# Sample attention of a streaming encoder: head-by-head products in four 32-column groups, keys turned three half-streams ahead

## The reference

```python
def diff_attn_sample(q, k_new, v_new, cache_k, cache_v, lam):
    s_past = jnp.einsum('bqhcd,bkhcd->bhcqk', q, cache_k)      # 512 cached keys per stream
    s_new = jnp.einsum('bqhcd,bkhcd->bhcqk', q, k_new)         # 16 new keys
    p = jax.nn.softmax(jnp.concatenate([s_past, s_new], axis=-1), axis=-1)
    a = p[:, :, 0] - lam * p[:, :, 1]                          # the two maps c = 0, 1
    return (jnp.einsum('bhqk,bkhv->bqhv', a[..., :P], cache_v)
            + jnp.einsum('bhqk,bkhv->bqhv', a[..., P:], v_new))
```

## Time and profile before

| | us |
|---|---|
| median of three runs | 3280.58 |
| span of the profiled execution (the page gives no other time of it) | 3277.7 |
| PE busy | 3119.9 (95%) |
| PE weight loads busy | 2657.1 (81%) |
| DVE busy | 1301.2 (40%) |
| ACT busy | 853.0 (26%) |
| POOL busy | 767.1 (23%) |
| of the chain that ended last: PE | 31% of the span |
| of it L1645, L1610, L1597, L1629, L1617 (the sample stage) | 2%, 2%, 1%, 1%, 0% |

### The profile page before, as it was taken

One profiled execution on the slowest core, in us unless ns is written; L12 is line 12 of the kernel. 1 busy time (PEld: TensorE's weight loads), 2 busy tenths in 40 slices (PEclk: granted clock), 3 DMA queues, 4 the chain that ended last, 5 costly groups with the idle time before them and its releaser, 6 DMA issues. The chain is left out here.

```text
span 3277.7 us, 40419 instructions
## 1 busy us (share of the span) xinstructions
PE 3119.9 (95%) x15436; PEld 2657.1 (81%) x15436; DVE 1301.2 (40%) x2469; ACT 853.0 (26%) x1712; POOL 767.1 (23%) x895
## 2 busy tenths in 40 slices
PE   8999899899999999999998898899899999999997
PEld 6978577789998899978886777666678998899996
DVE  2156744532222222265224767633253222222226
ACT  2152331222211122221012555522123221122212
POOL 1112111421222121242121533412042211211214
PEclk9999888999999999999997988999898999999998
DMA  4102305111111111112224323253211111111111
GB/s 130 39 26 68 106 15 204 33 52 39 45 45 38 39 51 38 45 33 74 100 90 113 89 70 73 97 206 141 99 52 40 51 39 45 45 38 38 45 32 58
DMA packets 234007, 219.68 MB, mean 67 GB/s; under 512 B 78209, under 2 KB 178434, under 8 KB 233874
## 3 DMA queue, kind: packets, MB, share of 16 engines
q1 hardware_dynamic: 233874, 217.91, 21.1%
HBM read 184.83 MB, written 33.03 MB: 66 GB/s over the span
## 5 line engine op out<-in xcount | busy, mean ns | idle before, releaser
L1243 PE MATMUL ps<-xt,wsplit 128*128 128x384 f32 x5184 | 911.3, 336 | 2.4 <-DVE xt L1681 2.4
L1243 PEld LDWEIGHTS ps<-xt,wsplit 128*128 128x128 f32 x5184 | 907.8, 189 | 5.3 <-issue 2.0
L707 POOL TENSOR_TENSOR wsplit<-raw,wsplit 128x1024 fp32r<-128x1024 f32 x192 | 461.6, 2405 | 1837.6 <-ACT wsplit L881 1837.6
L1414 PE MATMUL ps<-wsplit,hT 128*128 128x512 f32 x3456 | 787.9, 390 | 0.0
L1414 PEld LDWEIGHTS ps<-wsplit,hT 128*128 128x128 f32 x3456 | 649.4, 188 | 134.1
L1261 PE MATMUL ps<-wsplit,xt 128*128 128x512 f32 x3024 | 703.6, 394 | 2.8 <-DVE xt L1681 2.8
L1261 PEld LDWEIGHTS ps<-wsplit,xt 128*128 128x128 f32 x3024 | 571.4, 190 | 128.4 <-issue 6.5
L881 ACT ACTIVATE wsplit<-raw 128x1024 fp32r<-128x1024 f32 x192 | 202.4, 1054 | 970.3 <-PE ps L1414 612.9
L1887 DVE TENSOR_TENSOR x_res<-x_res,ps 128x512 f32<-128x512 f32 x252 | 172.4, 687 | 439.3 <-PE ps L1414 439.3
L1920 DVE TENSOR_SCALAR hsq<-ps 128x384 f32<-128x384 f32 x192 | 107.1, 558 | 558.9 <-PE ps L1243 558.9
L1024 ACT ACTIVATE hsq<-hsq 128x384 f32<-128x384 f32 x192 | 101.1, 527 | 569.3 <-DVE hsq L1920 569.3
(11 more groups left out here) (169 smaller groups left out, 2526.1 us busy)
## 6 DMA issues: line engine op xcount, KB each, us to landing
raw<-in_w_up SPq DMA_DIRECT2D x64, 512.0 KB, 4.0
raw<-in_w_down SPq DMA_DIRECT2D x64, 512.0 KB, 3.7
Kc<-in_cache_k SPq DMA_DIRECT2D x8, 2048.0 KB, 9.4
Vc<-in_cache_v SPq DMA_DIRECT2D x8, 2048.0 KB, 8.1
raw<-in_w_in_a SPq DMA_DIRECT2D x24, 512.0 KB, 3.6
out<-kvs SPq DMA_DIRECT2D x36, 256.0 KB, 2.0
raw<-in_w_kv SPq DMA_DIRECT2D x16, 512.0 KB, 4.3
kqd<-out SPq DMA_DIRECT2D x128, 64.0 KB, 2.1
```

The costliest lines, as they stand in the source:

```text
L707: nc.gpsimd.tensor_tensor(wsplit[:, slot, 1, :], raw[:, slot, :], wsplit[:, slot, 0, :].bitcast(F32), ALU.subtract).then_inc(lo_done, 1)
L1243: last = nc.tensor.matmul(ps[0:M, b, 0:GW], st, xt[:, c, k, ng * GW:(ng + 1) * GW], start=(k == 0 and i == 0), stop=(k == KT - 1 and i == 2))
L1414: last = nc.tensor.matmul(ps[:, (v + t) % 6, :], hT[:, a, 2 * kp + k, tok:tok + P], wsplit[:, q, b, k * 512:(k + 1) * 512], start=(kp == 0 ...
```

## The change

Qbd shrinks to 32 columns a head, and POOL fills it with two copies for a stream instead of eight. Each score product has 32 output columns and writes its own 32 partitions of the bank, each closed by itself; the same for the new keys. The values become 20 products of 32 output columns and 128 value columns for a half-stream, each head with its own values only, into 128 columns of bank 3, beside the turned weights of the new keys; DVE copies them with one instruction. As bank 3 is now shared, weights2 of w waits for the outputs of w-1 (`smp_out`), and values2 doesn't any more. Bank 7 becomes a third bank for turned keys (K_BANK), KTb has room for three half-streams, keys are turned three ahead, and the orders of PE, ACT and DVE change. POOL's and SyncE's don't. The two-bank interleaving of turning and scores is gone: PE does scores of w+1, values of w-1, keys of w+3, weights of w.

```diff
-    Qbd = at("Qbd", O_V, [P, 2, H_B, P])
-    KTb = at("KTb", O_V + 8192, [P, 2, 4, 512])
+    Qbd = at("Qbd", O_V, [P, 2, H_B, 32])
+    KTb = at("KTb", O_V + 2048, [P, 3, 4, 512])
...
+    K_BANK = (4, 5, 7)
...
             for c in range(2):
-                for hh in range(4):
-                    col = 32 * hh + 16 * c
-                    nc.gpsimd.tensor_copy(Qbd[c * HD:(c + 1) * HD, b % 2, hh::4, col:col + 16],
-                                          QTs[c * HD:(c + 1) * HD, hh::4, b * 16:b * 16 + 16]).then_inc(smp_q_blocks, 1)
-
-                pool.wait_ge(smp_q_blocks, 8 * b + 4 * (c + 1))
+                nc.gpsimd.tensor_copy(Qbd[c * HD:(c + 1) * HD, b % 2, :, 16 * c:16 * c + 16],
+                                      QTs[c * HD:(c + 1) * HD, :, b * 16:b * 16 + 16]).then_inc(smp_q_blocks, 1)
+                pool.wait_ge(smp_q_blocks, 2 * b + c + 1)
...
-                if w >= 2:
-                    act.wait_ge(smp_s_full, w - 1)
-                nc.scalar.activation(KTb[:, w % 2, hh, :], ps[:, 4, :], ACT.Copy).then_inc(keys_copied0, 1)
+                if w >= 3:
+                    act.wait_ge(smp_s_full, w - 2)
+                nc.scalar.activation(KTb[:, w % 3, hh, :], ps[:, K_BANK[(4 * w + hh) % 3], :], ACT.Copy).then_inc(keys_copied0, 1)
 
         act.wait_ge(smp_qk_copied, 4)
-        cache_keys(0)
-        cache_keys(1)
+        for w in range(3):
+            cache_keys(w)
         exps2(0)
         for w in range(2 * STREAMS):
-            if w + 2 < 2 * STREAMS:
-                cache_keys(w + 2)
             if w + 1 < 2 * STREAMS:
                 exps2(w + 1)
+            if w + 3 < 2 * STREAMS:
+                cache_keys(w + 3)
             weights2(w)
...
+        def cache_keys(w):
             b, z = w // 2, w % 2
+            if z == 0:
                 pe.wait_ge(kc_in[b % 2], 16 * (b // 2 + 1))
+            for hh in range(4):
+                n = 4 * w + hh
+                if n >= 3:
+                    pe.wait_ge((keys_copied0, keys_copied1)[(n - 3) % 2], (n - 3) // 2 + 1)
+                for kt in range(4):
+                    last = nc.tensor.transpose(ps[:, K_BANK[n % 3], kt * P:(kt + 1) * P],
+                                               Kc[:, b % 2, kt, (4 * z + hh) * P:(4 * z + hh + 1) * P], ident)
+                last.then_inc(cache_turned, 1)
+
+        def scores2(w):
 
             b, z = w // 2, w % 2
+            pe.wait_ge(smp_q_blocks, 2 * (b + 1))
+            pe.wait_ge(keys_copied0, 2 * w + 2)
+            pe.wait_ge(keys_copied1, 2 * w + 2)
+            if w:
+                pe.wait_ge(smp_exp, 2 * w)
+            for hh in range(4):
+                nc.tensor.matmul(ps[32 * hh:32 * hh + 32, w % 2, :], Qbd[:, b % 2, 4 * z + hh, :],
+                                 KTb[:, w % 3, hh, :], start=True, stop=True)
+            for hh in range(4):
+                last = nc.tensor.matmul(ps[32 * hh:32 * hh + 32, 2, 0:16],
+                                        Qbd[:, b % 2, 4 * z + hh, :], KTn[:, 4 * z + hh, 16 * b:16 * b + 16],
+                                        start=True, stop=True)
+            last.then_inc(smp_s_full, 1)
 
         def weights2(w):
             pe.wait_ge(smp_exp, 2 * w + 2)
             pe.wait_ge(smp_select, w + 1)
             if w:
                 pe.wait_ge(smp_w_copied, w)
+                pe.wait_ge(smp_out, w)
...
-            if w:
-                pe.wait_ge(smp_out, w)
 
             for kt in range(5):
-                v = (Vc[:, b % 2, kt, :] if kt < 4 else vS)[:, z * 512:(z + 1) * 512]
-                last = nc.tensor.matmul(ps[:, 7, :], ATs[:, w % 2, kt, :], v, start=(kt == 0), stop=(kt == 4))
+                v = Vc[:, b % 2, kt, :] if kt < 4 else vS[:, :]
+                for hh in range(4):
+                    last = nc.tensor.matmul(ps[32 * hh:32 * hh + 32, 3, P:2 * P],
+                                            ATs[:, w % 2, kt, 32 * hh:32 * hh + 32],
+                                            v[:, (4 * z + hh) * P:(4 * z + hh + 1) * P],
+                                            start=(kt == 0), stop=(kt == 4))
             last.then_inc(smp_pv, 1)
...
+        for w in range(3):
+            cache_keys(w)
+        scores2(0)
+        for w in range(2 * STREAMS):
+            if w + 1 < 2 * STREAMS:
+                scores2(w + 1)
             if w:
                 values2(w - 1)
+            if w + 3 < 2 * STREAMS:
+                cache_keys(w + 3)
+            weights2(w)
         values2(2 * STREAMS - 1)
...
-            for hh in range(4):
-                last = nc.vector.tensor_copy(oW[32 * hh:32 * hh + 32, w, :],
-                                             ps[32 * hh:32 * hh + 32, 7, hh * P:(hh + 1) * P])
-            last.then_inc(smp_out, 1)
+            nc.vector.tensor_copy(oW[:, w, :], ps[:, 3, P:2 * P]).then_inc(smp_out, 1)
...
+        for w in range(3):
+            cache_keys(w)
         maxima2(0)
         for w in range(2 * STREAMS):
-            if w + 2 < 2 * STREAMS:
-                cache_keys(w + 2, 1)
             combination(w)
-            if w + 2 < 2 * STREAMS:
-                cache_keys(w + 2, 3)
             if w + 1 < 2 * STREAMS:
                 maxima2(w + 1)
             if w:
                 outputs2(w - 1)
+            if w + 3 < 2 * STREAMS:
+                cache_keys(w + 3)
             if w >= 3:
                 sample_norm(w - 3)
```

More of the change, by code:

```diff
@@ L166, in encoder_step @@
     KTn = at("KTn", O_XT + 69632, [P, H_B, P])
-    Qbd = at("Qbd", O_V, [P, 2, H_B, P])
-    KTb = at("KTb", O_V + 8192, [P, 2, 4, 512])
+    Qbd = at("Qbd", O_V, [P, 2, H_B, 32])
+    KTb = at("KTb", O_V + 2048, [P, 3, 4, 512])
     kqS = at("kqS", O_RAW + 8192, [P, 2, D])
-    PS = at("PS", O_V + 24576, [P, 2, 640])
-    ATs = at("ATs", O_V + 29696, [P, 2, 5, P])
+    PS = at("PS", O_V + 26624, [P, 2, 640])
+    ATs = at("ATs", O_V + 31744, [P, 2, 5, P])
     oW = at("oW", O_RAW, [P, 2 * STREAMS, P])
@@ L1167, in exps2 @@
                                  scale=HD ** -0.5, accum_out=ls[:, w % 2, 0:1]).then_inc(smp_exp, 1)
-            nc.scalar.activation(PS[:, w % 2, 512 + 16 * b:528 + 16 * b], ps[:, 2, 0:16], ACT.Exp,
+            nc.scalar.activation(PS[:, w % 2, 512 + 16 * b:528 + 16 * b],
+                                 ps[:, 2, 0:16], ACT.Exp,
                                  bias=nmx[:, w % 2, 0:1], scale=HD ** -0.5,
@@ L1586, in _ @@
         pe.wait_ge(smp_qk_copied, 4)
-        def cache_keys(w, hh):
+        def cache_keys(w):
             b, z = w // 2, w % 2
-            if z == 0 and hh == 0:
+            if z == 0:
                 pe.wait_ge(kc_in[b % 2], 16 * (b // 2 + 1))
[L1592 to L1599, removed]
@@ L1601, in scores2 @@
-        def scores2(w, hh):
-            b, z = w // 2, w % 2
[L1604 to L1612, removed]
-                if w:
[L1615 to L1620, removed]
+            for hh in range(4):
[6 more added lines that the diff above has]
+                last.then_inc(cache_turned, 1)
@@ L1639, in values2 @@
                 pe.wait_ge(vc_in[b % 2], 16 * (b // 2 + 1))
-            if w:
-                pe.wait_ge(smp_out, w)
             for kt in range(5):
-                v = (Vc[:, b % 2, kt, :] if kt < 4 else vS)[:, z * 512:(z + 1) * 512]
-                last = nc.tensor.matmul(ps[:, 7, :], ATs[:, w % 2, kt, :], v, start=(kt == 0), stop=(kt == 4))
-            last.then_inc(smp_pv, 1)
-        for hh in range(4):
-            cache_keys(0, hh)
-        for w in range(-1, 2 * STREAMS):
-            for hh in range(4):
-                if w + 2 < 2 * STREAMS:
[L1653 to L1658, removed]
+                v = Vc[:, b % 2, kt, :] if kt < 4 else vS[:, :]
[4 more added lines that the diff above has]
+                                            start=(kt == 0), stop=(kt == 4))
+            last.then_inc(smp_pv, 1)
+        for w in range(3):
[4 more added lines that the diff above has]
+                scores2(w + 1)
             if w:
                 values2(w - 1)
+            if w + 3 < 2 * STREAMS:
+                cache_keys(w + 3)
+            weights2(w)
         values2(2 * STREAMS - 1)
@@ L2160, in _, with cache_keys @@
                                       ps[:, 2 * i + z, :].rearrange("p (k n) -> p k n", n=P)).then_inc(smp_qk_copied, 1)
[L2162 to L2166, removed]
+        def cache_keys(w):
+            for hh in (1, 3):
+                dve.wait_ge(cache_turned, 4 * w + hh + 1)
+                if w >= 3:
+                    dve.wait_ge(smp_s_full, w - 2)
+                nc.vector.tensor_copy(KTb[:, w % 3, hh, :], ps[:, K_BANK[(4 * w + hh) % 3], :]).then_inc(keys_copied1, 1)
         def maxima2(w):
```

## The result

The changed kernel takes 3189.91 us (median of three runs, 3183.74 to 3194.04), a ratio of 0.9722 to the kernel before (95% interval 0.9697 to 0.9747): 90.7 us less. The forecast was 3210 us, with a range of 3193 to 3235.

The account below looks back on a forecast made before the run. PE alone bounds the sample streams' attention. Start +1.6, thirteen iterations of 6.8 instead of 11.49 us -61.0, end -9.9, last copy -0.9: -70.2 us, a span of 3207.5, forecast 3210 us as spans lie 2.9 below the median; range 3193 to 3235.

Parts of the forecast that it names:

- an iteration under 5.9 us: Sample streams' attention: the prediction called itself wrong if an iteration took over 7.6 or under 5.9 us.
- start to the end of weights(0): Start of the stage: first scores wait for stream 1's keys, so weights(0) end at 2139.9 instead of 2138.3, +1.6 us.
- iteration 13: Last of thirteen full iterations in the sum, each forecast at 6.8 us instead of 11.49.
- iterations 14, 15, last values: End of the stage: 5.3 us for iteration 14, 8.0 for the rest, 13.3 for 23.2, so -9.9 us.
- the values: Values products on PE: 40 records at 0.05 us each, 2.0 us an iteration instead of 4.29, bounds 1.1 and 4.8.
- rows 3: Earlier profile's rows of the scan's 64-column products, two groups streaming at once, with 0.055 us extra a pass.
- floor: Chain of scores, maxima, exp, ACT's key copy, fourth key tile and weights: at least 6.15 us an iteration.
- A: Rival: two passes of a product hold back the next, only neighbours overlap; iteration 8.25 us, 3230 us in all; chance 0.15.
- B: Rival: no overlap in 32-column groups; iteration 12.0 us, 3289 us in all; chance 0.04.
- C: Rival: PE's clock falls in the stage; 3226 us in part (chance 0.05), 3298 in full (0.04).
- D: Rival: keys come late, a stream's loads need 16.4 us instead of 13.6; iteration 8.2, 3230 us; chance 0.06.
- at a 75% share: Key and value loads: 10.3 us a stream at 409 GB/s against 2 x 6.8 = 13.6 us, so they fit.

Follow-up runs that it names:

- e6: The changed kernel with copies of turned keys swapped, DVE taking tiles 0 and 2, ACT tiles 1 and 3: 3186.61 us, ratio 0.972.
- e4: The changed kernel with all four heads' products written to the same partitions 0 to 31: 3275.55 us (one run).
- e5: The changed kernel with POOL's sample_rstd one half-stream later: 3191.57 us, ratio 0.9731.
- e8: The changed kernel with the first scores ahead of the third half-stream's key turning: 3187.86 us, ratio 0.9727.
- e9: The changed kernel with the edits of e6 and e8 together: 3180.55 us, ratio 0.970.
- e1: The kernel before with the 32-column products alone, in its old interleaved order with two key banks: 3228.21 us, ratio 0.9841.
- e2: The kernel before with the new order alone, 128-column products, two key banks, keys two ahead: 3293.81 us, ratio 1.0045.
- e7: e6 with the edit of e5, loading only 128 of 512 cached values per stream from the third stream on: 3182.32 us (one run).

## Why the prediction was wrong in size

The stage should have lost 70.2 us and lost 91.2. The prediction's own sign of being wrong, an iteration under 5.9 us, is there: 5.74. By the steps of the sum:

| step | predicted | measured | difference |
|---|---|---|---|
| start to the end of weights(0) | +1.6 | -0.45 (20.02 to 19.57) | -2.1 |
| iterations 1 to 12 | 12 x 6.8 | 12 x 5.74 | -12.7 |
| iteration 13 | 6.8 | 4.0 | -2.8 |
| iterations 14, 15, last values | 13.3 | 10.1 | -3.2 |
| last copy and what follows | -0.9 | -1.15 | -0.25 |

**The iteration: the mis-sized term is the values.** I had 1.1 + 0.4 + 2.0 + 2.1 + 1.2 = 6.8; measured are 0.88 + 0.06 + 1.21 + 2.35 + 1.21 = 5.71. Values give 0.79 of the 1.1 us, new keys 0.34, scores 0.22; the key turning takes 0.26 more, since the wait for ACT's copy stands in it. I took 0.05 us a record because no row showed a faster row of records; 40 records in 1.21 us are 0.03 each, and even the 0.055 a pass that I carried over from the 64-column pairs of the earlier trace rows was not there: ten passes of 0.108 alone are 1.08. In the changed kernel the second passes of the scores start 0.45 us after the first ones, where 0.43 is their own length. Between bounds of 1.1 and 4.8 the value lies at the lower one. The step from rows 3 was sound in kind (full overlap), and the caution that I added to it was the error. The same terms make most of the difference at the end.

**The floor was no floor.** The prediction gave 6.15 us as a floor "even if the products cost less", and the lower end of the range hung on it. But its first term was the 1.5 us of scores, one of these products. The other links were right to 0.12 us in all: forecast were 4.65 us from the end of the scores on, measured are 4.77. With scores and new keys of 0.94 instead of 1.5, the prediction's own chain is 5.6, and measured it is 5.71. The prediction did name 5.7 us and 3194, but put it down to a shorter chain on ACT; that chain wasn't shorter, the scores were, so the near hit is luck. Maxima begin 0.26 behind the scores, exp 1.24 later, ACT's copy 0.92 later, the fourth tile 0.65, weights 0.49, and 1.21 to the end. e6 shows that this chain, and not PE's own work, was the bound: with ACT's copy taken out of it, the half-stream falls to 5.30. So PE's own work is 5.3 us at most, where the sum had 6.8.

**Iteration 13.** I kept thirteen iterations with key turning from before; turning three ahead leaves twelve, and the one moved is in the start. That is a plain miscount. By the prediction's own terms an iteration without keys takes 5.3 us (its iteration 14), so 1.5 of the 2.8 us are the miscount, and the rest are the products again.

**The start.** The keys of stream 1 landed 7.8 us after their issue, not 9.4, and the scores were shorter. The chain after has that transfer:

```profile
2122.88 7.79 DMA Kc<-in_cache_k
```

**The rivals.** A (passes hold each other back) is refuted by 0.88 us for eight records. B is refuted by the change and priced by e4, 3275.55 us, where I had 3289: in one strip the new keys (0.25 us, not 0.8) and the values (4.46, not 4.8) cost less than I thought. C: the clock was 1.00 in all iterations from 1 on. D: no wait in the iterations of the changed kernel, but the room was 11.1 us and not 14.5, and e5, e8 and e9 each ran into it. The transfers "at a 75% share" were worked out for 6.8 us from 409 GB/s; by the same sum they need 10.3 of 11.5 us at 5.74, a share of 0.9, and the profile shows 1.0 at 352 to 392 GB/s. No run of the changed kernel shows them as the bound of an iteration.

What was right: PE alone bound the stage before, the four strips overlap fully, order and width of products belong together (e1, e2), the copy of tile 0 behind exp is what is late next, and POOL's clearing is level with it.

The four scores are faster than the 2.38x of the Trainium skill would make them ("TensorE: Matmul & The Clock Gate", Part 3, measured there with three strips): 3.44/0.88 = 3.9 with four. The page also states that weight loads overlap only where row groups differ; here all strips use all rows, and all eight weight loads of the scores are done by 2176.73, while the first passes stream until about 2177.0, so the measurement decides.

```profile
2176.57 0.16 PEld L1610 LDWEIGHTS ps<-KTb,Qbd 128*32 128x32 f32 x8
```

## What to carry to other kernels

Products of 32 output columns, each to its own 32-partition strip, ran four abreast in fp32 where they stood next to each other in PE's queue; with full-width work between them nothing was left of the gain (the scores of e1). When a term shrinks fourfold, recompute every "hidden" and every "floor" with the small value as well, down to the queue of the transfers: what had 14 us of room had 11, and the loads took 10.6. Count the iterations that still hold the moved step.

## What the runs showed of the hardware

Four strips stream at once at the price of one: 0.88 us for eight records of 512 columns, 1.21 us for forty of 128 (0.03 us each), against 3.46 and 4.46 in one strip (e4). A change from full-width to 32-column work and back costs 0.26 us a pair (e1). The transfers ran at a share of 1.0 with anything from 353 (the changed kernel) to 411 GB/s (e6), while PE stayed at clock 1.00 in both: the share alone doesn't say how much more they could move. The same waits of PE, 1.25 and 0.85 us, stood ahead of a fall of the clock to 0.50 in e5 and ahead of none in e7.
